# 48 modulation units: weighted sums of weight chunks on VectorE and a sum over partitions on TensorE, in place of matrix products

## The chip, the cores and the metric

One core (a NeuronCore) of one Trainium2 chip runs the whole kernel. The metric is the device time of one execution in microseconds; the median of three executions of the kernel before is 2996.09 us (2994.24 to 2999.81). The profile is of one further execution.

## The reference, cut to what matters

The program is a two-layer block with modulated norms, followed by a second two-layer block that the change does not touch. In each layer of the first block, two condition vectors (`c` and `c_ctx`, 1024 values each) give nine modulation vectors each:

```
def _modulation(cond, w, b):
    m = jax.nn.silu(cond) @ w + b        # w is 1024 x 9216
...
sh1, sc1, g1, shm, scm, gm, sh2, sc2, g2 = _modulation(c, ada_w[layer], ada_b[layer])
csh1, csc1, cg1, cshm, cscm, cgm, csh2, csc2, cg2 = _modulation(c_ctx, ada_w[layer], ada_b[layer])
h = h + 0.5 * g1 * _swiglu(_prenorm(h, norm_ffn1[layer], sh1, sc1), ffn1_w_in[layer], ffn1_w_out[layer])
...
h = h + gm * (mix_l @ mix_w_out[layer])
h = h + 0.5 * g2 * _swiglu(_prenorm(h, norm_ffn2[layer], sh2, sc2), ffn2_w_in[layer], ffn2_w_out[layer])
```

`_swiglu` is a feed-forward stage: first products (`h @ w_in`, the gate and the other half), silu of the gate times the other half, second products (`@ w_out`).

## The kernel before, in words

**Products.** Activations lie with features on partitions, 256 latent and 256 context tokens beside each other (512 columns). Every float32 product is done as three matmuls of the type fp32r: high part times high part, low times high, high times low (`three`, L470 to L472). Weights come through the double-buffered tile `raw` in *units*: a unit is one slot `s` (0 or 1) with two halves. SP loads each half (L379), ScalarE copies it to the high part `whi` (L412), VectorE subtracts to get the low part `wlo` (L419), TensorE multiplies. The semaphores `lo_ready`, `mm_done` and `evac_done` link them, so that loads run about two units ahead and splits one unit ahead. `pairs_of` (L422) writes the loop over pairs of units for each compute engine: in each unit first `before`, then `ahead` (the split of the next unit), then the body.

**A feed-forward stage** (`ffn`, one function for each engine) goes over the 22 blocks of 128 hidden features in two parts of 12 and 10 (`HALVES`). A part has first products (`up`, one unit for each hidden block: 8 chunks x 2 x 3 = 48 matmuls of 512 columns) and second products (`down`, 8 units, that is four pairs). In an `up` unit ScalarE takes the silu of the gate (L2065), VectorE multiplies (L2749), ScalarE copies the high part of the hidden block (L2068), VectorE subtracts for the low part (L2753). In `down` VectorE adds the product, scaled by the modulation, to `hT` (L2800).

**Modulation units.** A layer's 9216 modulation columns are 36 units of 256 columns, 72 in all. Eight are computed in the opening, 16 in three stretches about the norms (`MOD_AT_NORM`), and 48 beside the products of the feed-forward stages (`MOD_BESIDE`): in feed-forward 1 and feed-forward 2 of layer 0, in six groups of 5, 4, 1, 5, 4 and 5 pairs of units, beside `up` and `down` pairs. These 48 are the subject. For each, SP loads 1 MB of `ada_w` into a slot of `mod_w` (L723) as soon as TensorE is through with that slot. At the start of a pair of product units, TensorE waits for both loads and runs `mod_rows_of` (L558) for both slots: for each of eight chunks of 128 input features one float32 matmul, with 32 columns of `cond` (the two conditions, placed so that they meet the rows of this unit) as the loaded operand and 256 weight columns streaming. The eight go by turns to the four groups of 32 rows of the PSUM bank 6. At a group's end VectorE copies the bank to `mod_row` (L2623), TensorE turns rows to columns (`mod_turned`, L565), which also adds the four row groups, and VectorE adds the bias (L2546).

**Order on SP's queue.** `sp_units` (L369) issues, for each unit, the two halves of `raw`, each behind its wait, and then the modulation load of this slot with its own wait (`mod_unit`, L718). In the last `down` of a stage `mods_at_norm` puts one load for the next norm behind each pair.

Of the kernel before, what the change touches and what calls it, by code (L numbers as in the profile page):

```python
# [26 lines left out]
P = 128  # L27
D = 1024
DC = D // P
T = 256  # L30
# [93 lines left out]
def build(nc, io, const_at):  # L124

    ctx = ExitStack()
    with ctx:
# [56 lines left out]
        out_at = first.at  # L184
        mod_w = first("mod_w", [P, 2, DC, 2 * P])
        mod_row = first("mod_row", [P, 2 * P])
        mod_w2 = first("mod_w2", [P, DC, 2 * P])
        mod_w3 = Region(out_at - 4 * 4 * 2 * T)("mod_w3", [P, DC, 2 * P])
        normed = Region(overlay)("normed", [P, DC, 2 * T])
# [359 lines left out]
        def mod_landings(layer, m0):  # L549

            before = [part[2] for stage in ("ffn1", "ffn2") for part in beside_parts[stage] if part[:2] < (layer, m0)]
            return 16 * (sum(before) + 1)
# [9 lines left out]
        def mod_turned(row, bank):  # L562
# [5 lines left out]

        beside_parts = {stage: [part for part in MOD_BESIDE[stage] if part] for stage in ("ffn1", "ffn2")}
        mod_groups = [2] * (MOD_FIRST // 2) + [2 * part[2] for part in beside_parts["ffn1"]] + \  # L570
            [MOD_AT_NORM[name][2] for name in ("mix", "ffn2")] + [2 * part[2] for part in beside_parts["ffn2"]] + \
            [MOD_AT_NORM["ffn1"][2]]
# [60 lines left out]
        none = (None,) * 4  # L633
        beside = {(stage, 0): mods for stage, mods in MOD_BESIDE.items()}
        for layer, mixer, w_in in ((0, "even", io["even_w_in"][0]), (1, "odd", io["odd_w_in"][0])):
# [10 lines left out]
                 beside.get(("ffn1", layer), none), False, PAIR if layer else OPENING,  # L646
# [8 lines left out]
                 beside.get(("ffn2", layer), none), False, 0 if layer else PAIR, None if layer else "ffn1"),  # L655
# [30 lines left out]
        def _(sp):  # L686
# [50 lines left out]
            def ffn(w_in, w_out, mods, opened, at_norm):  # L737
                v = w_in.rearrange("(c p) (g f) -> p c g f", p=P, g=2)
                j0 = 0
                for n, half in enumerate(HALVES):  # L740
# [4 lines left out]
                    for p0, pairs, mod_part in parts(half // 2, mods[2 * n], p_first):  # L745
                        sp_units(sp, c, pairs, up(p0), UNIT, mod_part and mod_unit(*mod_part))
                    if n == 1 and at_norm:
# [7 lines left out]
                    for p0, pairs, mod_part in parts(4, mods[2 * n + 1]):  # L755
                        sp_units(sp, c, pairs, columns(w_out, j0, half, 2 * p0 * P, P, P), half * P,
                                 mod_part and mod_unit(*mod_part))
# [114 lines left out]
        def _(pe):  # L872
# [41 lines left out]
            def opening():  # L914
# [51 lines left out]
                for t in range(1, (n_rows + P - 1) // P):  # L966
# [6 lines left out]
                    .then_inc(S("bcast_mm"), 1)  # L973

            def mod_unit(layer, m0, pairs):
                group = mod_group(layer, m0)
                def rows_first(i, s):
                    if s:
                        return
                    if i == 0:  # L980
                        pe.wait_ge(S("mod_copied"), group)
                    for slot in range(2):
                        pe.wait_ge(S(f"mod_landed{slot}"), 16 * i + mod_landings(layer, m0))
                        mod_rows_of(mod_w[:, slot, :, :], 6, 2 * i + slot, 2 * pairs).then_inc(S("mod_rows_mm"), 1)
# [1518 lines left out]
        def _(dve):  # L2503
# [227 lines left out]
            def ffn(n_tok, final, mods, gate, scaled=False, opened=0, at_norm=None, turned=None):  # L2731
                for n, half in enumerate(HALVES):
# [34 lines left out]
                    for p0, pairs, mod_part in parts(half // 2, mods[2 * n], p_first):  # L2767
# [5 lines left out]
                        if mod_part:  # L2773
                            mod_read(*mod_part, pairs)
# [847 lines left out]
```

## Time and profile before

| | |
|---|---|
| median of three runs | 2996.09 us |
| the profiled execution's own time | 2992.23 us |
| its span, first to last instruction | 2990.5 us |
| TensorE matmul, busy | 2932.5 us, 98% |
| VectorE, busy | 1690.7 us, 57% |
| ScalarE, busy | 1314.1 us, 44% |
| moved by DMA | 439.36 MB, mean 147 GB/s |

The profiled execution took 1.7 us more than its span. Matmuls are pipelined, so a matmul's listed duration is longer than the distance from one start to the next; costs on TensorE are best read from distances of starts.

### The profile page before, as it was taken

Reading aid. Unit: us, or ns where it says so; the run is one execution under the profiler, and the core shown is the slowest. Engines: PE = TensorE matmul, PEld = TensorE weight load, DVE = VectorE, ACT = ScalarE, POOL = GpSimd, SP = SyncE. Lnnn points to the kernel's source line nnn. Section 1 sums busy time; section 2 is a strip of 40 time slices with the busy share of each in tenths; the row PEclk is TensorE's granted clock in tenths of the full one; section 3 lists DMA queues with packets and bytes.
Section 4 is the critical chain, followed back from the end, with each engine's and each line's share of the span. In section 5 each row is a group of like instructions: output and inputs, shape, how many; then the busy total and the mean of one; then the engine's idle time right before and its main releaser. Section 6 shows DMA issues by size and latency. Waiting matters only on the chain.

```text
span 2990.5 us, 52037 instructions
## 1 busy us (share of the span) xinstructions
PE 2932.5 (98%) x20172; PEld 2580.5 (86%) x20172; DVE 1690.7 (57%) x2664; ACT 1314.1 (44%) x1952; POOL 0.2 (0%) x4
## 2 busy tenths in 40 slices
PE   9999999999999999999998999999999999999999
PEld 6778878787777878888888999999899999988998
DVE  4333363545332453334666667677776776777766
ACT  4322343423222342223335656555555555556555
POOL 0000000000000000000000000000000000000000
PEclk9999999999999999999999999999999999999999
DMA  9555343146566433332322666455446654554564
GB/s 275 181 176 148 89 154 93 43 149 176 166 202 181 141 113 95 95 105 76 121 85 79 190 184 186 132 156 170 141 141 196 175 156 146 166 164 139 163 191 137
DMA packets 639011, 439.36 MB, mean 147 GB/s; under 512 B 22172, under 2 KB 627192, under 8 KB 638712
## 3 DMA queue, kind: packets, MB, share of 16 engines
q1 hardware_dynamic: 637844, 436.70, 49.1%
q8 instruction: 125, 2.05, 0.3%
q14 instruction: 46, 0.38, 0.0%
q10 hardware_dynamic: 996, 0.23, 0.0%
HBM read 430.84 MB, written 1.05 MB: 144 GB/s over the span
## 4 chain that ended last, share of the span: by engine, by line
PE 87%; DVE 8%; ACT 1%; issue 1%; SPq 1%; DMA 1%; DVEq 0%; ACTq 0%
PE ps L470 26%; PE ps L472 25%; PE ps L471 25%; DVE wlo L419 2%; PE ps L558 2%; ACT whi L412 1%; DMA raw<-ffn_w_in 1%; PE ps L1809 1%; DVE normed L2684 1%; PE ps L1789 1%; SPq L734 1%; PE ps L1821 1%; DVE xl L2676 1%; PE ps L1270 0%; PE ps L1279 0%
## 5 line engine op out<-in xcount | busy, mean ns | idle before, releaser
L470 PE MATMUL ps<-xh,whi 128*128 128x256 f32 (+1 forms) x3744 | 1204.8, 322 | 24.4 <-DVE wlo L419 5.6
L471 PE MATMUL ps<-xl,whi 128*128 128x256 f32 (+1 forms) x3744 | 1183.7, 316 | 0.0
L472 PE MATMUL ps<-xh,wlo 128*128 128x256 f32 (+1 forms) x3744 | 1183.6, 316 | 0.0
L419 DVE TENSOR_TENSOR wlo<-raw,whi 128x1024 fp32r<-128x1024 f32 x732 | 869.1, 1220 | 182.7 <-ACT whi L412 174.5
L412 ACT ACTIVATE whi<-raw 128x1024 fp32r<-128x1024 f32 x731 | 747.4, 1053 | 462.1 <-PE ps L472 398.9
L470 PEld LDWEIGHTS ps<-xh,whi 128*128 128x128 f32 x3744 | 705.4, 188 | 106.5 <-issue 45.0
L472 PEld LDWEIGHTS ps<-xh,wlo 128*128 128x128 f32 x3744 | 705.6, 188 | 50.6
L471 PEld LDWEIGHTS ps<-xl,whi 128*128 128x128 f32 x3744 | 706.3, 189 | 48.6
L470 PE MATMUL ps<-hid_h,whi 128*128 128x512 f32 (+1 forms) x1056 | 353.4, 335 | 0.0
L471 PE MATMUL ps<-hid_l,whi 128*128 128x512 f32 (+1 forms) x1056 | 352.3, 334 | 0.0
L472 PE MATMUL ps<-hid_h,wlo 128*128 128x512 f32 (+1 forms) x1056 | 352.2, 334 | 0.0
L2749 DVE TENSOR_TENSOR hid<-act,ps 128x512 f32<-128x512 f32 (+1 forms) x132 | 73.2, 554 | 440.0 <-PE ps L472 429.0
L2068 ACT ACTIVATE hid_h<-hid 128x256 f32 (+3 forms) x132 | 69.3, 525 | 426.2 <-DVE hid L2749 426.2
L470 PEld LDWEIGHTS ps<-hid_h,whi 128*128 128x128 f32 x1056 | 198.8, 188 | 23.9 <-issue 3.3
L472 PEld LDWEIGHTS ps<-hid_h,wlo 128*128 128x128 f32 x1056 | 198.5, 188 | 20.7
L471 PEld LDWEIGHTS ps<-hid_l,whi 128*128 128x128 f32 x1056 | 198.2, 188 | 20.4
L2800 DVE SCALAR_TENSOR_TENSOR hT<-ps,mod,hT 128x256 f32 (+1 forms) x112 | 49.8, 480 | 212.8 <-PE ps L472 212.4
L2753 DVE TENSOR_TENSOR hid_l<-hid,hid_h 128x256 f32 (+3 forms) x132 | 73.8, 559 | 105.6 <-ACT hid_h L2068 105.6
L2065 ACT ACTIVATE act<-ps 128x512 f32<-128x512 f32 (+1 forms) x88 | 47.5, 540 | 148.7 <-PE ps L472 148.6
L470 PE MATMUL ps<-whi,xh 128*128 128x256 f32 x384 | 110.7, 288 | 0.1
L472 PE MATMUL ps<-whi,xl 128*128 128x256 f32 x384 | 107.5, 280 | 0.0
L471 PE MATMUL ps<-wlo,xh 128*128 128x256 f32 x384 | 107.5, 280 | 0.0
(380 smaller groups left out, 2593.9 us busy)
## 6 DMA issues: line engine op xcount, KB each, us to landing
raw<-ffn_w_in SPq DMA_DIRECT2D x176, 512.0 KB, 4.7
mod_w<-ada_w SPq DMA_DIRECT2D x72, 1024.0 KB, 7.7
raw<-w_in SPq DMA_DIRECT2D x96, 512.0 KB, 4.6
raw<-w_ffn_in SPq DMA_DIRECT2D x88, 512.0 KB, 4.7
raw<-w_gate SPq DMA_DIRECT2D x64, 512.0 KB, 4.1
raw<-ffn_w_out SPq DMA_DIRECT2D x64, 384.0 KB, 3.9
raw<-ffn_w_out SPq DMA_DIRECT2D x64, 320.0 KB, 3.6
raw<-w_branch SPq DMA_DIRECT2D x32, 512.0 KB, 3.4
```

The source lines that it names most:

```text
L412: nc.scalar.activation(split_at(unit_of(u, i), whi, s, h), raw[:, s, h, :], ACT.Copy).then_inc(S("hi_ready"), 1)
L419: nc.vector.tensor_tensor(split_at(unit, wlo, s, h), raw[:, s, h, :], split_at(unit, whi, s, h).bitcast(F32), ALU.subtract).then_inc(S("lo ...
L470: nc.tensor.matmul(dst, w_h, x_h, start=start, stop=False)
L471: nc.tensor.matmul(dst, w_h, x_l, start=False, stop=False)
L472: return nc.tensor.matmul(dst, w_l, x_h, start=False, stop=stop)
L558: m = nc.tensor.matmul(ps[g, bank, 0:2 * P], cond[:, k, 30 - 2 * j:62 - 2 * j], w[:, k, :], start=j == 0 and k < 4, stop=j == n - 1 and k ...
L734: sp.dma_start(norm_tiles[name][j], mod_columns((MOD_UNITS * layer + m0 + j) // MOD_UNITS, (m0 + j) % MOD_UNITS))\
L2065: nc.scalar.activation(act32[:, s, 0:n_tok], gate_in, ACT.Silu).then_inc(S("act_ready"), 1)
L2068: nc.scalar.activation(hid_h[:, bass.ds(i * 2 + (hid0 + s), 1), 0:n_tok], hid32[:, s:s + 1, 0:n_tok], ACT.Copy).then_inc(S("hid_h_ready"), 1)
L2749: nc.vector.tensor_tensor(hid32[:, s, 0:n_tok], act32[:, s, 0:n_tok], ps[:, 2 * s + 1, 0:n_tok], ALU.mult).then_inc(S("evac_done"), 1)
L2753: nc.vector.tensor_tensor(hid_l[:, to, 0:n_tok], hid32[:, s:s + 1, 0:n_tok], hid_h[:, to, 0:n_tok].bitcast(F32), ALU.subtract)\
L2800: ins = nc.vector.scalar_tensor_tensor(out=hT[:, to, sl], in0=ps[:, 2 * s:2 * s + 1, sl], scalar=mod[:, bass.ds(i * 2 + (gate0 + n0 + s), ...
```

## The change

The 48 units are computed by another route, and all of them beside *first* products: five pairs in each part of feed-forward 1 and of feed-forward 2 of layer 0, and four pairs in the first part of feed-forward 1 of layer 1. Which units are computed about the third norm is changed to suit (24 to 27 of layer 1 in place of 32 to 35).

For a pair of units (512 weight columns), SP loads half of the input features of both units at a time (`mod_pair`, again 1 MB for each DMA, 48 in all, now with runs of 512 columns). VectorE multiplies each of the eight chunks by the condition's value of that partition and adds, once for each condition: 16 instructions of 128x512 for a pair, eight in each unit of the product pair, four before the split of the next unit and four after it. TensorE then multiplies the accumulated tiles by a column of ones: four matmuls for a pair. Their place is one pair later, ahead of its second unit; the last pair's are ahead of the first `down` unit, and the rows are turned ahead of the second.

```
-MOD_BESIDE = {"ffn1": ((0, 8, 5), (0, 18, 4), (0, 26, 1), None),
-              "ffn2": ((1, 4, 5), (1, 14, 4), (1, 22, 5), None)}
-MOD_AT_NORM = {"mix": (0, 28, 4, 3, 4), "ffn2": (0, 32, 8, 5, 6), "ffn1": (1, 32, 4, 3, 4)}
+MOD_BESIDE = {("ffn1", 0): ((0, 8, 5), (0, 18, 5)), ("ffn2", 0): ((1, 4, 5), (1, 14, 5)), ("ffn1", 1): ((1, 28, 4), None)}
+MOD_AT_NORM = {"mix": (0, 28, 4, 3, 4), "ffn2": (0, 32, 8, 5, 6), "ffn1": (1, 24, 4, 3, 4)}
+MOD_STEPS = 2 * DC
...
+        mod_sel = first("mod_sel", [P, 2 * 32])
+        mod_pair = Region(mod_w_at)("mod_pair", [P, DC, 4 * P])
+        mod_acc = Region(mod_acc_at)("mod_acc", [P, 2, 2, 4 * P])
```

In the stream of SP:

```
             def mod_unit(layer, m0):
...
+                sp.wait_ge(S("mod_rows_mm"), MOD_UNITS * layer + m0)
+                before = c.of["mod_pairs"]
                 def load(i, s):
-                    sp.wait_ge(S("mod_rows_mm"), 2 * i + (MOD_UNITS * layer + m0 + s - 1))
-                    sp.dma_start(mod_w[:, s, :, :], mod_columns(layer, i * 2 + (m0 + s))).then_inc(S(f"mod_landed{s}"), 16)
+                    sp.wait_ge(S("mod_step"), i * MOD_STEPS + mod_summed(before - 1, DC * (s + 1)))
+                    sp.dma_start(mod_pair[:, s * DC // 2:(s + 1) * DC // 2, :], mod_pair_columns(layer, i * 2 + m0, s))\
+                        .then_inc(S(f"mod_landed{s}"), 16)
```

In the stream of TensorE (the former `rows_first` and `turned` go):

```
             def mod_unit(layer, m0, pairs):
...
+                def rows(pair):
+                    if pair == 0:
+                        pe.wait_ge(S("mod_copied"), group)
+                    pe.wait_ge(S("mod_step"), mod_summed(before + pair, MOD_STEPS))
+                    for u in range(2):
+                        for j in range(2):
+                            to, g = 2 * (2 * pair + u) + j, 32 * (2 * u + j)
+                            m = nc.tensor.matmul(ps[g:g + 32, 6, 0:2 * P], mod_sel[:, 31 - to:63 - to],
+                                                 mod_acc[:, pair % 2, j, u * 2 * P:(u + 1) * 2 * P],
+                                                 start=pair == 0, stop=pair == pairs - 1)
+                    m.then_inc(S("mod_rows_mm"), 2)
+                def rows_before(i, s):
+                    if s == 1 and i:
+                        rows(i - 1)
```

In the stream of VectorE:

```
+            def mod_sums(layer, m0):
...
+                def sums(i, s, part):
+                    pair = before + i
+                    if part == 0:
+                        dve.wait_ge(S(f"mod_landed{s}"), 16 * (pair + 1))
+                    if s == 0 and part == 0:
+                        dve.wait_ge(S("mod_rows_mm"), MOD_UNITS * layer + m0 + max(0, 2 * (i - 1)))
+                    for k in range(4 * s + 2 * part, 4 * s + 2 * part + 2):
+                        for j in range(2):
+                            acc, weight = mod_acc[:, i % 2, j, :], cond[:, k, 30 + j:31 + j]
+                            if k == 0:
+                                ins = nc.vector.tensor_scalar(acc, mod_pair[:, k, :], weight, None, ALU.mult)
+                            else:
+                                dve.wait_ge(S("mod_step"), mod_summed(pair, 2 * k + j - 1))
+                                ins = nc.vector.scalar_tensor_tensor(out=acc, in0=mod_pair[:, k, :], scalar=weight,
+                                                                     in1=acc, op0=ALU.mult, op1=ALU.add)
+                            ins.then_inc(S("mod_step"), 1)
```

VectorE runs `sums(i, s, 0)` as `before` of each `up` unit and `sums(i, s, 1)` at the start of its body, ahead of the multiplication L2749. At the first `down` unit it copies the rows, waits for the turned ones, adds the bias, and halves the gate. Two memsets prepare `mod_sel` in each stage. The waits of SP for `mod_rows_mm` now stand at the entry of a group, ahead of the raw loads of its first pair.

## Rows read from the trace of the kernel before

**Rows 1.** The page: busy us (share) xinstructions, and the granted clock.
```profile
PE 2932.5 (98%) x20172; PEld 2580.5 (86%) x20172; DVE 1690.7 (57%) x2664; ACT 1314.1 (44%) x1952; POOL 0.2 (0%) x4
...
PEclk9999999999999999999999999999999999999999
```
**Rows 2.** The page: the chain of work that ended last, by engine.
```profile
PE 87%; DVE 8%; ACT 1%; issue 1%; SPq 1%; DMA 1%; DVEq 0%; ACTq 0%
```
**Rows 3.** Groups by shape, TensorE: busy us, mean ns | idle before.
```profile
L558 PE MATMUL ps<-mod_w,cond 128*32 128x256 f32 x1152 | 70.0, 383 | 1.4 <-DMA mod_w<-ada_w 1.4
```
**Rows 4.** Timeline of VectorE, feed-forward 1: start us, us, instruction [idle before].
```profile
109.23 0.69 DVE L2749 TENSOR_TENSOR hid<-act,ps 128x512 f32<-128x512 f32 x1 [6.07 <-PE ps L472]
110.84 0.69 DVE L2753 TENSOR_TENSOR hid_l<-hid,hid_h 128x512 f32 x1 [0.92 <-ACT hid_h L2068]
...
133.08 0.69 DVE L2749 TENSOR_TENSOR hid<-act,ps 128x512 f32<-128x512 f32 x1 [6.08 <-PE ps L472]
...
171.49 0.69 DVE L2753 TENSOR_TENSOR hid_l<-hid,hid_h 128x512 fp32r<-128x512 f32 x1 [0.80 <-ACT hid_h L2068]
172.09 0.42 DVE L2623 COPY mod_row<-ps 128x256 f32<-128x256 f32 x1
```
**Rows 5.** The same view in layer 1, no modulation beside.
```profile
1129.32 0.69 DVE L2749 TENSOR_TENSOR hid<-act,ps 128x512 f32<-128x512 f32 x1 [6.07 <-PE ps L472]
...
1131.77 2.36 DVE L419 TENSOR_TENSOR wlo<-raw,whi 128x1024 fp32r<-128x1024 f32 x2
...
1151.08 0.69 DVE L2749 TENSOR_TENSOR hid<-act,ps 128x512 f32<-128x512 f32 x1 [6.07 <-PE ps L472]
```
**Rows 6.** Timeline of TensorE: groups of 4, 16 and 32 small matmul records.
```profile
49.59 0.39 PE L472 MATMUL ps<-xh,wlo 128*128 128x512 f32 x1
49.82 0.53 PE L565 MATMUL ps<-consts,mod_row 128*128 128x32 f32 x4
50.18 0.48 PE L470 MATMUL ps<-xh,whi 128*128 128x512 f32 x1
...
62.29 1.07 PE L558 MATMUL ps<-mod_w,cond 128*32 128x256 f32 x16 [0.76 <-DMA mod_w<-ada_w]
63.29 0.50 PE L470 MATMUL ps<-xh,whi 128*128 128x512 f32 x1
...
85.28 1.93 PE L558 MATMUL ps<-mod_w,cond 128*32 128x256 f32 x32
87.14 0.50 PE L470 MATMUL ps<-xh,whi 128*128 128x512 f32 x1
```
**Rows 7.** Groups by shape, VectorE: nearest forms to the new instructions.
```profile
L3055 DVE SCALAR_TENSOR_TENSOR o_p<-o_p,o_st 128x512 f32<-128x512 f32 x12 | 9.0, 752 | 0.4
...
L3053 DVE TENSOR_SCALAR o_p<-o_p,o_st 128x512 f32<-128x512 f32 x12 | 5.8, 487 | 0.4
```
**Rows 8.** Timeline of VectorE: spacing of unchained instructions, and (last) of chained ones.
```profile
34.71 1.26 DVE L2572 SCALAR_TENSOR_TENSOR normed<-hT,gains,ps 128x256 f32<-128x256 f32 x3
...
1522.60 0.75 DVE L3055 SCALAR_TENSOR_TENSOR o_p<-o_p,o_st 128x512 f32<-128x512 f32 x1
1523.27 1.22 DVE L3062 TENSOR_REDUCE o_st<-ps 128x2 f32<-128x1024 f32 x1
...
1863.63 1.51 DVE L3199 SCALAR_TENSOR_TENSOR m_cv<-m_in,vec,m_cv 128x255 f32<-128x255 f32 x3
```
**Rows 9.** All instructions of `mod_w`: landing of its loads.
```profile
DMA to landing us min/median/max: 5.0/7.7/12.3
```
**Rows 10.** Timeline of SP's queue in the opening: start, time over the group.
```profile
33.69 6.02 SPq L379 DMA_DIRECT2D raw<-ffn_w_in  x2
48.61 0.37 SPq L723 DMA_DIRECT2D mod_w<-ada_w  x1
```
**Rows 11.** Timeline of ScalarE, first split of the first unit after the opening.
```profile
55.57 1.06 ACT L412 ACTIVATE whi<-raw 128x1024 fp32r<-128x1024 f32 x1
```
**Rows 12.** The page: DMA issues of `raw`, KB each, us to landing.
```profile
raw<-ffn_w_in SPq DMA_DIRECT2D x176, 512.0 KB, 4.7
```

More of the change, by code:

```diff
@@ L631, in build @@
         schedule = []
-        none = (None,) * 4
-        beside = {(stage, 0): mods for stage, mods in MOD_BESIDE.items()}
+        none = (None,) * 2
         for layer, mixer, w_in in ((0, "even", io["even_w_in"][0]), (1, "odd", io["odd_w_in"][0])):
@@ L754, in ffn @@
                         continue
-                    for p0, pairs, mod_part in parts(4, mods[2 * n + 1]):
-                        sp_units(sp, c, pairs, columns(w_out, j0, half, 2 * p0 * P, P, P), half * P,
-                                 mod_part and mod_unit(*mod_part))
+                    sp_units(sp, c, 4, columns(w_out, j0, half, 0, P, P), half * P)
                     j0 += half
@@ L972, in opening, with rest @@
                 nc.tensor.matmul(ps[:, 5, 64:128], K("ones")[0:1, :], small_rows[0:1, :], start=True, stop=True)\
-                    .then_inc(S("bcast_mm"), 1)
+                    .then_inc(S("vec_t"), 1)
             def mod_unit(layer, m0, pairs):
-                group = mod_group(layer, m0)
-                def rows_first(i, s):
-                    if s:
-                        return
[L980 to L984, printed above, removed]
-                def turned(i, s):
-                    if i == pairs - 1 and s == 1:
+                group, before = mod_group(layer, m0), c.of["mod_pairs"]
+                c.add(mod_pairs=pairs)
+                def rows(pair):
[12 more added lines that the diff above has]
+                        rows(i - 1)
+                def rest(i, s):
+                    if not isinstance(i, int) or i:
+                        return
+                    if s == 0:
+                        rows(pairs - 1)
+                    else:
                         pe.wait_ge(S("mod_copied"), group + 1)
@@ L2766, in ffn @@
                         late_vectors()
-                    for p0, pairs, mod_part in parts(half // 2, mods[2 * n], p_first):
+                        dve.wait_ge(S("cond"), 1)
+                    if mods[n] and n == 0:
+                        link(nc.vector.memset(mod_sel[:, :], 0.0))
+                        link(nc.vector.memset(mod_sel[:, 31:32], 1.0))
+                    for p0, pairs, mod_part in parts(half // 2, mods[n], p_first):
                         hid0 = 2 * p0
                         split_done = n == 0 and not gate
+                        sums = mod_sums(*mod_part) if mod_part else None
@@ new lines, in ffn, with down @@
+                    add = add_gated(gate, n_tok // T, 0) if gate else add_plain(n, 0)
+                    def down(i, s):
+                        if mods[n] and is_first(i, s):
+                            mod_copy_and_read(mods[n][0], mods[n][1], mods[n][2])
+                            if n == 0:
+                                gate_halved()
+                        unit_done(dve, c, i, s)
+                        add(i, s)
+                        if n == 1:
+                            sq_lag(i, s, 1, n_tok)
@@ L2791, in ffn @@
+                    pairs_of(dve, c, 4, down, ahead=dve_split, final=final and n == 1, first=n == 1 or bool(mods[n]))
                 sq_close(1, n_tok)
```

107 lines of the change are left out of this document (52 added, 55 removed).

## The prediction

> **What bounds the kernel now.** I read the busy shares first: TensorE is busy 98% of the span, at a granted clock in the top tenth in every slice (the 2.4 GHz level), while VectorE has 43% free [rows 1]. The chain of waits says the same: 87% of it lies on TensorE [rows 2]. So whatever leaves TensorE's stream comes off the time, unless another engine then makes it wait. The groups by shape show what the change takes hold of: 1152 records of L558, 70 us busy, only 1.4 us of waiting for their loads [rows 3]. They are 72 units of 8 matmuls with 2 records each; the 48 units in question are 768 of them.
>
> **What a pair of units costs TensorE now.** The timeline of VectorE is a clean ruler, since L2749 starts when a unit of products ends. Over one pair with modulation it goes from 109.23 to 133.08, 23.85 us [rows 4]; over one without, from 1129.32 to 1151.08, 21.76 us [rows 5]. A pair of units costs 2.09 us, of which 1.86 is seen directly (85.28 to 87.14, 32 records [rows 6]) and 0.23 is the change-over to and from the fp32r products. 24 pairs: 50.2 us, all on the path. The pair after the opening also waits 0.76 us for its load [rows 6].
>
> **What a pair costs TensorE after.** 4 matmuls of the same shape, 8 records, one in each of the same four row groups. The trace has no group of 8. Sixteen records take 1.00 us to the next product (62.29 to 63.29), thirty-two 1.86 [rows 6], so one more record is 0.054 us and eight would be 1.86 - 24 x 0.054 = 0.57; with the change-over of 0.23, 0.80. From below the bound is a quarter of 2.09, 0.52; from above the 16-record group with change-over, 1.23. I take 0.80, between rows of the same shape: 19.2 us for 24 pairs (12.5 to 29.5). Groups beside products fall from six to five, so one turning of 4 records goes: 49.82 to 50.18, 0.4 us [rows 6]. Sum on TensorE: -50.2 - 0.8 + 19.2 - 0.4 = **-32.2 us** (-22 to -39).
>
> **What VectorE gets.** For each pair 2 multiplications by a scalar and 14 multiply-and-add of 128x512. Nearest rows: 752 ns for the same operation and width, 487 ns for the multiplication [rows 7]. They overlap by some 0.08 us: the 752 ns instruction is followed 0.67 us later, and three unchained ones of 256 columns take 1.26 us where the three chained in m_cv take 1.51, 0.12 us more for each link [rows 8]. The new sums alternate between two accumulators and wait only for the last but one, which is done by then; I take 0.67 and 0.40: 14 x 0.67 + 2 x 0.40 = 10.2 us a pair, 5.1 a unit, 5.4 where all eight are sums. Fully chained it would be 0.79 each, 6.3 a unit. From below, 0.67 is already the spacing of an unhindered one.
>
> The Trainium skill has a rule that speaks against counting on the overlap: "VectorE: DVE Perf Modes", section "The DRAIN you can't avoid", says that the next operation does not start until the pipe is empty, and that semaphores cost nothing extra. By that rule a sum would take its full 0.75 us, some 6.0 us for eight. The trace disagrees in both halves (0.67 apart, and 0.12 for a link [rows 8]); the verdict below holds at either price.
>
> A unit's round on VectorE: L2749 to L2753 1.61 us (109.23 to 110.84), L2753 to the next 0.60 [rows 4], the two splits 2.36 [rows 5], together 4.6; with 5.4 of sums 10.0 us. TensorE's round is 10.88 us (half of 21.76), 11.28 with half of the 0.80. VectorE would be near 90% busy in these stretches, but still the faster one. Order matters as well as sum. With t=0 where TensorE ends the last unit: L2749 and L2753 until 2.2, four sums until 4.9, the splits until 7.3, four sums until 10.0, then the wait for the unit's end at 10.9 or 11.7. The next unit's split is due at 10.9, so 3.6 us of slack; fully chained sums leave 3.1. The first two chunks of a row group are needed a unit later. Only a group's last pair is short: TensorE wants it right at the end of the last `up` unit (11.7), VectorE is done at 10.0; chained, 10.9. Cost nil in both.
>
> **Loads and SP's queue.** Still 48 DMAs of 1 MB, in place of L723's. Each half of `mod_pair` is a single buffer: it is reloaded when its eight sums are done (t=10.0 of one unit) and wanted two units on, at 2.2: 22.6 + 2.2 - 10.0 = 14.8 us, against a landing of 7.7 us in the median and 12.3 at most [rows 9]. On SP the raw loads of a slot stand behind the modulation load before them, hence are issued near t=10 instead of t=7.3; ScalarE wants them a unit later, landing takes 4.7 us [rows 12]. Nil. The new wait at a group's entry holds raw loads back: those of the first unit after the opening were issued at 33.69 and now follow at about 48.6, where the wait for the rows is released [rows 10]. Landed by 48.6 + 0.5 + 4.7 = 53.8, they precede ScalarE's split at 55.57 [rows 11]; if that cover of 1.8 us is gone, each further us is a us once. At the last `down` of two stages the modulation loads now wait for rows made at the first `down` unit, and the raw load behind them too; the unit they serve is two `down` units away, 13.6 us (30 matmuls each at 10.88/48). Later groups' waits are long fulfilled. After the opening VectorE comes late to the second unit's split, behind two memsets and the first four sums (2 x 0.40 + 2 x 0.67 = 2.1 us): between nothing and 2.1 us once, and I count 0.5, since TensorE has a whole unit of 10.9 us to run first. At the first `down` unit VectorE waits for the turned rows, until just after that unit's end; its split is done before, and the bank is wanted only a unit (8.2 us, 36 matmuls) later. Nil. TensorE's first `down` row groups are in the 24. What is late next, after the removed wait for a load, is the split.
>
> **Sum.** -32.2 + 0.5 = -31.7 us on the execution profiled: 2992.2 to 2960.5. The median of the runs shown stands 3.9 us higher, so by it 2964.4; I say **2964**. A measurement of this kernel can tell about 0.2%, 6 us, from no change.
>
> **The rivals.**
>
> *Small row groups cost more than their records* (chance 0.08). If 8 records cost like 16, the pair costs 1.23 and the sum is -21.5: 2974. For it: entering from fp32r costs something regardless of size. Against: the 4-record group took only 0.36 us [rows 6].
>
> *VectorE falls a little behind* (0.14). The sums stand ahead of split and L2749. It decides where a sum takes more than (11.28 - 4.6) / 8 = 0.84 us. At 0.90 a round is 11.8 and each of some 46 units loses 0.5: 23 us of the gain, 2987 (2970 to 2994). For it: such a density of dependent 512-column work is nowhere in the trace. Against: 0.79 even when chained.
>
> *The loads become the bound, and it is slower* (0.09). The head of VectorE's queue now waits for the modulation load, and behind that wait stand the split and L2749, hence ScalarE and TensorE; before, TensorE alone waited. The loop is: load, sums over two sections with the split between (7.8 us), load again. The pair takes 22.6 us while the load lands within 14.8; each us beyond costs one for each of the 19 pairs that follow another in their group. It eats the whole gain at 16.5 us; at 18 us it is 3.2 x 19 - 32 = +29: **3025**. For it: the opening shows loads of up to 12.3 us. Against: the median of 7.7, and the same bytes in almost the same time.
>
> *As forecast* 0.69 (2957 to 2970).
>
> The change that doesn't do what it says (sums stay on TensorE) isn't possible by the diff; the nearest case is the first rival.
>
> **How the numbers follow.** The first two cases lie at 2957 to 2975 with 0.77; a mild lag of VectorE reaches to 2984, with some 0.07 of its 0.14. Below, the quarter bound gives -39, 2957. So 2956 to 2984 holds a bit over 8 in 10. Faster by over 0.2%: 0.69 + 0.08 + 0.10 of the lag = 0.87; within 0.2%: 0.04, the heavy end of the lag; slower: 0.09.
>
> **What would show it.** TensorE's small matmuls drop from 1152 records to 384 of the old form and 192 of the new; their new groups take about 0.57 us to the next product. L2749 starts 22.6 us apart over two units. The new sums are 750 ns long and 0.67 apart; VectorE's busy time rises by some 24 x 11.5 = 276 us (durations, less the overlap). Idle of L470 on `wlo` L419 stays where it was: if it grows by more than 5 us, the lag is real. If VectorE's first sum of a section waits for the `mod_pair` load, the third rival is at work. A time above 2984 would say that I misjudged a wait on VectorE.

## The result, and the profile after

| | before | changed |
|---|---|---|
| median, runs on the same chip | 2997.79 us (2994.24 to 2999.81) | 2969.7 us (2962.13 to 2971.68, four runs) |
| the profiled execution | 2992.23 us, span 2990.5 | 2962.13 us, span 2960.3 |

The ratio of the times is 0.9908, with a 95% interval of 0.9895 to 0.9922: by it 27.6 us less (23.4 to 31.5). The two profiled executions are 30.1 us apart; both are fast ones, that of before faster than the four runs of the table, that of the changed kernel the fastest of its four. The forecast was 31.7 us less for the profiled execution and 2964 for the median; the measured median is 5.7 us above that and inside the range.

The page of the changed kernel: the span, busy us and counts as in [rows 1], the chain by engine as in [rows 2], and the new issue of loads (KB each, us to landing).

```profile
span 2960.3 us, 51063 instructions
...
PE 2901.3 (98%) x19592; PEld 2559.7 (86%) x19592; DVE 1928.7 (65%) x3052; ACT 1314.6 (44%) x1952; POOL 0.2 (0%) x4
...
PE 86%; DVE 8%; ACT 2%; issue 1%; SPq 1%; DMA 1%; DVEq 0%; ACTq 0%
...
mod_pair<-ada_w SPq DMA_DIRECT2D x48, 1024.0 KB, 5.3
```

TensorE is busy 31.2 us less and still 98% of the span: what it lost came off the end. VectorE gained 238 us of work and the chain's share on it stayed at 8%. The groups by shape (busy us, mean ns | idle before) show where both sit; the first line answers to [rows 3].

```profile
L566 PE MATMUL ps<-mod_w,cond 128*32 128x256 f32 x384 | 23.7, 390 | 0.3 <-DMA mod_w<-ada_w 0.3
...
L995 PE MATMUL ps<-mod_acc,mod_sel 128*32 128x256 f32 x192 | 15.3, 391 | 0.0
...
L2656 DVE SCALAR_TENSOR_TENSOR mod_acc<-mod_pair,cond,mod_acc 128x512 f32<-128x512 f32 x336 | 230.7, 746 | 0.0
...
L2653 DVE TENSOR_SCALAR mod_acc<-mod_pair,cond 128x512 f32<-128x512 f32 x48 | 21.0, 481 | 0.1
```

Old records: 384 instead of 1152. New ones: 192, and the engine never stood idle for them (0.0). The sums took 746 ns and never waited for a load either; the multiplications ahead of them waited 0.1 us in all. One new group in TensorE's timeline, answering to [rows 6]:

```profile
91.40 0.39 PE L477 MATMUL ps<-xh,wlo 128*128 128x512 f32 x1
91.72 0.64 PE L995 MATMUL ps<-mod_acc,mod_sel 128*32 128x256 f32 x8
92.29 0.50 PE L475 MATMUL ps<-xh,whi 128*128 128x512 f32 x1
```

From the group's start to the next product it is 92.29 - 91.72 = 0.57 us, the interpolated value. VectorE's timeline over a pair (L2788 is the former L2749, L2792 the former L2753, L424 the split), as in [rows 4]:

```profile
91.93 0.69 DVE L2788 TENSOR_TENSOR hid<-act,ps 128x512 f32<-128x512 f32 x1 [1.53 <-PE ps L477]
...
94.03 2.74 DVE L2656 SCALAR_TENSOR_TENSOR mod_acc<-mod_pair,cond,mod_acc 128x512 f32<-128x512 f32 x4
96.68 2.35 DVE L424 TENSOR_TENSOR wlo<-raw,whi 128x1024 fp32r<-128x1024 f32 x2
98.95 2.73 DVE L2656 SCALAR_TENSOR_TENSOR mod_acc<-mod_pair,cond,mod_acc 128x512 f32<-128x512 f32 x4
103.61 0.69 DVE L2788 TENSOR_TENSOR hid<-act,ps 128x512 f32<-128x512 f32 x1 [1.93 <-PE ps L477]
...
114.49 0.69 DVE L2788 TENSOR_TENSOR hid<-act,ps 128x512 f32<-128x512 f32 x1 [1.66 <-PE ps L477]
```

From 91.93 to 114.49 is 22.56 us: 21.76 of products [rows 5] and 0.80 for the new group with its change-over. VectorE's own work in a round is 103.61 - 1.93 - 91.93 = 9.75 us, after which it waits for TensorE. The forecast had 10.0.

**Where the time went, by stage.** The view of windows, us of the stretch first; then busy us of TensorE matmul, its loads, VectorE, ScalarE and GpSimd, granted clock, DMA share and GB/s. The stretches are: opening and feed-forward 1 of layer 0; the mixer; its output product with the norm sum; feed-forward 2 of layer 0; feed-forward 1 of layer 1. Before:

```profile
0.00:425.00 425.00, 417.52 (x2223) 331.46 (x2227) 164.88 (x233) 142.94 (x176) 0.20 (x4) 1.00 0.58 176
425.00:635.10 210.10, 202.71 (x1513) 172.23 (x1506) 108.32 (x215) 80.12 (x116) 0.00 (x0) 1.00 0.19 57
635.10:680.70 45.60, 45.22 (x270) 36.02 (x272) 20.81 (x34) 11.74 (x17) 0.00 (x0) 1.00 0.93 277
680.70:1079.40 398.70, 397.93 (x2168) 316.13 (x2160) 153.05 (x207) 118.61 (x149) 0.00 (x0) 1.00 0.57 172
1079.40:1448.90 369.50, 366.46 (x1637) 302.72 (x1627) 150.64 (x200) 117.72 (x148) 0.00 (x0) 1.00 0.32 94
```

Changed:

```profile
0.00:409.80 409.80, 403.20 (x1977) 322.55 (x1980) 263.83 (x393) 142.90 (x176) 0.20 (x4) 1.00 0.62 182
409.80:621.50 211.70, 204.34 (x1513) 173.34 (x1506) 108.31 (x215) 80.12 (x116) 0.00 (x0) 0.99 0.19 56
621.50:668.60 47.10, 45.29 (x271) 36.07 (x273) 20.83 (x34) 11.76 (x17) 0.00 (x0) 1.00 0.81 246
668.60:1047.90 379.30, 378.46 (x1796) 305.13 (x1788) 252.15 (x368) 119.16 (x149) 0.00 (x0) 1.00 0.54 158
1047.90:1420.90 373.00, 370.04 (x1669) 303.42 (x1662) 190.83 (x267) 117.63 (x147) 0.00 (x0) 1.00 0.41 119
```

Differences: -15.2, +1.6, +1.5, -19.4, +3.5, and -2.2 over the rest of the kernel, which the change does not touch; together -30.2. That rest took 1541.8 us before and between 1539.5 and 1548.6 us in the profiled executions of the changed kernel and its variants, so -2.2 is scatter, and some 9 us of scatter lie there. By the forecast's own prices the three feed-forward stages should give:

- first (10 pairs by the new route where 10 were by the old, one turning less, the load wait of 0.76 gone, +0.5 in the opening): -10 x 1.29 - 0.4 - 0.76 + 0.5 = -13.6;
- second (10 by the new where 14 were by the old): 10 x 0.80 - 14 x 2.09 - 0.4 = -21.7;
- third (4 new, one turning more): 4 x 0.80 + 0.4 = +3.6.

The third fits to 0.1 us. What the other stretches differ by has three causes, which the traces show.

*Short drops of the granted clock.* The mean clock of such long stretches is too coarse for them. In slices of 5 us both traces have some. One slice of before (25 to 30 us) and two stretches of the changed kernel:

```profile
25.00:30.00 5.00, 4.57 (x19) 2.73 (x22) 0.64 (x2) 1.36 (x2) 0.00 (x0) 0.67 1.10 303
```

```profile
520.00:530.00 10.00, 10.00 (x35) 7.29 (x35) 5.53 (x8) 7.08 (x9) 0.00 (x0) 0.83 0.35 107
665.00:675.00 10.00, 8.11 (x77) 5.25 (x70) 6.63 (x16) 5.66 (x11) 0.00 (x0) 0.83 0.01 2
```

The 0.67 and 0.83 are the granted clock: part of the slice at the 1.2 GHz level. As an estimate from them, each costs up to (1 - 0.67) x 5 or (1 - 0.83) x 10 = 1.7 us. The other profiles bear the first two out. The mixer took 211.7 or 211.8 us in the five profiles that had one such drop in it, 213.3 in the one with two, and 210.1 or 210.2 us in the others: this is the mixer's +1.6. The first stage took 409.2 to 410.1 us in the changed kernel and in every variant whose work there is the same and that had no drop at 25 us; the one of experiment 2 with ten sums had it (0.68) and took 411.6 us. Before had it, and so lost the 1.6 us by which the changed kernel did better than the forecast. The third drop lies at the start of the second feed-forward stage; the kernel of experiment 5, without a drop there, took 378.3 us for that stage, 1.0 less.

*The first pair of a stage was cheaper than 2.09 us.* Also without the drop, the second stage is some 1.3 us short of the forecast (378.3 - 398.7 = -20.4 instead of -21.7). TensorE's timeline at the start of the feed-forward stage, in the kernel before with modulation beside, before in layer 1 with none, and in the changed kernel:

```profile
707.58 1.93 PE L558 MATMUL ps<-mod_w,cond 128*32 128x256 f32 x32
709.45 0.50 PE L470 MATMUL ps<-xh,whi 128*128 128x512 f32 x1
```

```profile
1107.21 0.49 PE L470 MATMUL ps<-xh,whi 128*128 128x512 f32 x1 [0.84 <-DVE hid L2749]
```

```profile
697.22 0.50 PE L475 MATMUL ps<-xh,whi 128*128 128x512 f32 x1 [0.76 <-DVE hid L2788]
```

Where nothing else is to be done there, TensorE waits about 0.8 us for `hid`. The old matmuls of the group's first pair stood in that wait: they took 1.86 us and spared 0.84, so they cost 1.0 us and taking them away gave back 1.0, not 2.09. That explains 1.1 of the 1.3 us.

*The norm's sums come later.* In the stretch of the output product TensorE waits for them (waits: total us, times, longest), in the changed kernel

```profile
PE ps L1044 <- DVE ss L2546: 1.8, 1, 1.8
```

where the kernel before has

```profile
PE ps L1023 <- DVE ss L2524: 0.4, 1, 0.4
```

These 1.4 us are the stretch's +1.5. On VectorE's queue the split of the next stage's weights stands ahead of the norm's last sums. It waits for ScalarE's copy, and that for the load of `raw`. ScalarE's waits in that stretch, before and changed:

```profile
ACT whi L412 <- DMA raw<-ffn_w_in: 4.2, 2, 3.5
```

```profile
ACT whi L417 <- DMA raw<-ffn_w_in: 5.7, 2, 4.9
```

So the load reaches ScalarE 1.5 us later in relation to the products, and all behind it is late by as much. Counted from the end of the stretch's products, SP issued it 0.6 us later; why, and where the other 0.9 us come from, no run shows. The drop at 665 to 675 us follows TensorE's wait: of the twelve profiles with a wait of 1.6 to 2.0 us there, ten have a drop behind it, and the kernel before, with 0.4 us, has none.

### The profile page after: what moved, and what is told of

Same layout as the page of the kernel before. It is cut to its first block, busy times and chain, and to the rows that moved or that the text cites. A ratio compares the mean times of both kernels' runs of the same rounds, so it can differ in the third digit from the quotient of the medians.

```text
span 2960.3 us, 51063 instructions
## 1 busy us (share of the span) xinstructions
PE 2901.3 (98%) x19592; PEld 2559.7 (86%) x19592; DVE 1928.7 (65%) x3052; ACT 1314.6 (44%) x1952; POOL 0.2 (0%) x4
## 4 chain that ended last, share of the span: by engine, by line
PE 86%; DVE 8%; ACT 2%; issue 1%; SPq 1%; DMA 1%; DVEq 0%; ACTq 0%
PE ps L475 27%; PE ps L477 25%; PE ps L476 25%; DVE wlo L424 2%; ACT whi L417 1%; DMA raw<-ffn_w_in 1%; PE ps L1831 1%; PE ps L1811 1%; SPq L744 1%; DVE normed L2721 1%; PE ps L1843 1%; DVE xl L2713 0%; PE ps L566 0%; PE ps L995 0%; PE ps L1292 0%
## 5 line engine op out<-in xcount | busy, mean ns | idle before, releaser
L424 DVE TENSOR_TENSOR wlo<-raw,whi 128x1024 fp32r<-128x1024 f32 x732 | 868.4, 1220 | 169.7 <-ACT whi L417 167.1
L417 ACT ACTIVATE whi<-raw 128x1024 fp32r<-128x1024 f32 x731 | 747.6, 1054 | 448.5 <-PE ps L477 379.7
L2656 DVE SCALAR_TENSOR_TENSOR mod_acc<-mod_pair,cond,mod_acc 128x512 f32<-128x512 f32 x336 | 230.7, 746 | 0.0
L2788 DVE TENSOR_TENSOR hid<-act,ps 128x512 f32<-128x512 f32 (+1 forms) x132 | 73.2, 554 | 202.5 <-PE ps L477 191.5
L2792 DVE TENSOR_TENSOR hid_l<-hid,hid_h 128x256 f32 (+3 forms) x132 | 73.8, 559 | 99.5 <-ACT hid_h L2090 99.5
```

The source lines that it names most:

```text
L417: nc.scalar.activation(split_at(unit_of(u, i), whi, s, h), raw[:, s, h, :], ACT.Copy).then_inc(S("hi_ready"), 1)
L424: nc.vector.tensor_tensor(split_at(unit, wlo, s, h), raw[:, s, h, :], split_at(unit, whi, s, h).bitcast(F32), ALU.subtract).then_inc(S("lo ...
L2656: ins = nc.vector.scalar_tensor_tensor(out=acc, in0=mod_pair[:, k, :], scalar=weight, in1=acc, op0=ALU.mult, op1=ALU.add)
L2788: nc.vector.tensor_tensor(hid32[:, s, 0:n_tok], act32[:, s, 0:n_tok], ps[:, 2 * s + 1, 0:n_tok], ALU.mult).then_inc(S("evac_done"), 1)
L2792: nc.vector.tensor_tensor(hid_l[:, to, 0:n_tok], hid32[:, s:s + 1, 0:n_tok], hid_h[:, to, 0:n_tok].bitcast(F32), ALU.subtract)\
```

## The experiments

Ratios are to the kernel before, run beside each kernel on the same chip, with 95% intervals. The changed kernel was taken again as a control, as it is:

> The changed kernel once more, as the measure for the run of paired rows beside it: 0.991 of the kernel before, as when it was first measured (0.9908).

2967.64 us (2965.92 to 2970.38, five runs), 0.9913 [0.9899, 0.9926]. Its stretches were 410.1, 210.1, 46.9, 380.0 and 373.0 us, against the 409.8, 211.7, 47.1, 379.3 and 373.0 of the first profile.

**1. Are the sums hidden?** They keep number, order and waits and are cut to one column. This leaves out all but the first of their columns, for chunks 1 to 7.

```
-ins = nc.vector.scalar_tensor_tensor(out=acc, in0=mod_pair[:, k, :], scalar=weight,
-                                     in1=acc, op0=ALU.mult, op1=ALU.add)
+ins = nc.vector.scalar_tensor_tensor(out=acc[:, 0:1], in0=mod_pair[:, k, 0:1], scalar=weight,
+                                     in1=acc[:, 0:1], op0=ALU.mult, op1=ALU.add)
```

> The 14 multiply-and-add instructions of each pair work on one column in place of 512 (so 511 of 512 columns of the modulation sums hold only the first chunk's product); all semaphores, loads and TensorE's matmuls stay. Theory (VectorE's sums are wholly hidden behind TensorE's products): the same time as the changed kernel, span 2960 +-2, L2788 still starts 22.6 us apart over two units. Rival (VectorE lags a little and some of the 32 us expected on TensorE is lost to it): faster than the changed kernel by 2 to 10 us, and TensorE's idle before the first matmul of a unit, 9.7 us for the 128x512 form, falls.

2966.25 us, 0.9911 [0.9893, 0.9929]. The group, then two instructions of VectorE's timeline:

```profile
L2656 DVE SCALAR_TENSOR_TENSOR mod_acc<-mod_pair,cond,mod_acc 128x1 f32<-128x1 f32 x336 | 51.7, 213 | 0.0
```

```profile
91.48 0.69 DVE L2788 TENSOR_TENSOR hid<-act,ps 128x512 f32<-128x512 f32 x1 [4.13 <-PE ps L477]
...
103.16 0.69 DVE L2788 TENSOR_TENSOR hid<-act,ps 128x512 f32<-128x512 f32 x1 [6.19 <-PE ps L477]
```

179 us less of work on VectorE turned into waiting for TensorE (4.1 and 6.2 us instead of 1.5 and 1.9), with no time gained. The median is 1.4 us under the control's and 3.5 under the changed kernel's first one, which is scatter: the five stretches are 409.3, 211.7, 47.0, 379.7 and 373.0 us, none more than 0.5 us off the changed kernel's, and TensorE's idle time before the first matmul of a unit, which the rival had falling, went from 9.7 to 10.1 us. The sums cost nothing. The rival in which VectorE lags is out at eight sums.

**2. Where does it begin to cost?** Further sums of the same form into the same accumulators: two in each unit (ten in all), or four (twelve), half of them ahead of the split. Their weight is a column of zeros, so the accumulated values stay, and only VectorE's work grows.

```
+MOD_EXTRA = 2
-MOD_STEPS = 2 * DC
+MOD_STEPS = 2 * DC + 2 * MOD_EXTRA
...
+dve.wait_ge(S("mod_step"), mod_summed(pair, n - 1))
+nc.vector.scalar_tensor_tensor(out=acc, in0=mod_pair[:, ks[0], :], scalar=cond[:, ks[0], 0:1],
+                               in1=acc, op0=ALU.mult, op1=ALU.add).then_inc(S("mod_step"), 1)
```

> Two more multiply-and-add of 128x512 in each unit (weight zero, so nothing changes in the result), ten in place of eight. From the changed kernel's trace a unit on VectorE is 2.1 us of hid work, 2.3 of splits and 0.66 for each sum: 11.0 us with ten sums (10.7 on average, the two multiplications of a pair being shorter), against TensorE's 11.28. Theory: still hidden, +0 to +3 us on the changed kernel. Rival (what stands in front on VectorE's queue costs, sum by sum): +15 us or more (48 units x 2 x 0.66 = 63 at worst).

> Four more multiply-and-add of 128x512 in each unit (weight zero), twelve in place of eight. A unit on VectorE becomes 12.1 us on average against TensorE's 11.28. Theory: past the crossing, some 0.8 us for each of 48 units less the slack of each group's first units, +25 to +37 us on the changed kernel, so level with the kernel before or a little slower (span 2985 to 2997), with TensorE idle before L475 on wlo or hid. Rival (sums cost nothing whatever their number, or each costs its full length): +0, or +127 us.

Ten: 2967.86 us, 0.9907 [0.9889, 0.9926], still free. Twelve: 3017.54 us, 1.0075 [1.0053, 1.0096]: slower than the kernel before, 48 us above the changed one and 50 above the control; the expectation of +25 to +37 was too low. VectorE's timeline with ten (L2798 is L2788 moved down):

```profile
96.47 0.68 DVE L2798 TENSOR_TENSOR hid<-act,ps 128x512 f32<-128x512 f32 x1
...
107.45 0.68 DVE L2798 TENSOR_TENSOR hid<-act,ps 128x512 f32<-128x512 f32 x1
...
117.90 0.68 DVE L2798 TENSOR_TENSOR hid<-act,ps 128x512 f32<-128x512 f32 x1
...
150.93 0.69 DVE L2798 TENSOR_TENSOR hid<-act,ps 128x512 f32<-128x512 f32 x1 [0.51 <-PE ps L478]
```

No wait stands behind the first three lines: VectorE goes at its own pace, 10.98 and 10.45 us a round (the second has the two cheaper multiplications), mean 10.7. TensorE needs 11.28 on average, so VectorE, which starts the stage late behind its first sums, catches up by 1.1 us a pair, and from 150.93 on it waits for TensorE again. The lag cost nothing: less its drop of the clock, the stage took the control's 410 us. With twelve the rounds are 12.31 and 11.79, mean 12.05, 0.77 us too long, and nothing is caught up. Over some 46 units that would be 35 us. TensorE's waits with twelve:

```profile
PE ps L996 <- DVE mod_acc L2658: 24.7, 4, 6.2
PE ps L476 <- DVE wlo L425: 20.7, 29, 1.5
```

The first line did not exist in the changed kernel; the second stood there at 8.8 us, 11.9 less. Together 36.6 us, the lag as worked out. The two profiled spans are further apart, 3014.6 - 2960.3 = 54.3 us. TensorE stood idle for 41.3 us more (the 36.6 and some smaller waits), and the same 19592 matmul records kept it busy for 13.0 us more, 2914.3 instead of 2901.3. The second part goes with the clock. The end of one group and the stretch behind it:

```profile
183.55 1.08 PE L996 MATMUL ps<-mod_acc,mod_sel 128*32 128x256 f32 x8 [6.20 <-DVE mod_acc L2658]
```

```profile
180.00:190.00 10.00, 6.45 (x26) 4.60 (x27) 7.48 (x11) 2.52 (x3) 0.00 (x0) 0.66 0.39 112
```

TensorE stood idle for 6.20 us, and the 10 us around it show a clock of 0.66; a slice at a lower clock stands at each of the four such waits. (1 - clock) x 5 us, summed over all slices of 5 us, gives 22.1 us, where the changed kernel's profile has 10.5. The 11.6 more are an upper estimate, since part of such a slice was idle anyway; the busy time is the better measure. The lag of a group's units gathers unseen, since buffers and a split a unit ahead cover it, and two thirds of it is paid at one place, the group's last rows, which are wanted at once.

**3. What does a small row group cost?** The four matmuls once more, with a column of zeros as the second loaded operand.

```
+for u in range(2):
+    for j in range(2):
+        g = 32 * (2 * u + j)
+        m = nc.tensor.matmul(ps[g:g + 32, 6, 0:2 * P], mod_sel[:, 32:64],
+                             mod_acc[:, pair % 2, j, u * 2 * P:(u + 1) * 2 * P],
+                             start=False, stop=pair == pairs - 1)
```

> Each pair's four row matmuls are followed by four more with an all-zero weight, in the same four row groups: 16 records for a pair in place of 8. Theory (price by records, 0.054 us each, plus 0.23 change-over for a group): +0.43 us for each of 24 pairs, +10.4 us on the changed kernel, each group 1.00 us to the next product. Rival (a group's price is its start and end, records overlap in the four row groups): +0 to +3 us. Other rival (eight matmuls cost twice four): +0.8 x 24 = +19 us.

2979.43 us, 0.9944 [0.9926, 0.9962]: 9.7 us above the changed kernel's median and 11.8 above the control's, or 0.41 to 0.49 us for each of 24 pairs (the forecast's slope: 8 x 0.054 = 0.43). A pair takes 12.15 + 10.88 us between starts of the multiplication, 0.47 more than in the changed kernel (11.68 + 10.88). In the timeline:

```profile
92.29 0.64 PE L995 MATMUL ps<-mod_acc,mod_sel 128*32 128x256 f32 x8
92.75 0.61 PE L1001 MATMUL ps<-mod_acc,mod_sel 128*32 128x256 f32 x8
93.29 0.50 PE L475 MATMUL ps<-xh,whi 128*128 128x512 f32 x1
```

Sixteen records take 1.00 us to the next product, as in [rows 6]. The price of records is straight, and eight records do not cost like sixteen: the first rival is out.

**4. The change-over by itself.** Rows of two pairs made together, every second pair, with a third pair of accumulators in a tile that is free there. The work is the same, the visits to TensorE's stream fewer: three instead of five in a group of five pairs, two instead of four in a group of four, 10 fewer in all.

```
+def acc_of(pair, j):
+    return sq2[:, j, :] if pair % 3 == 2 else mod_acc[:, pair % 3, j, :]
...
-if s == 1 and i:
+if s == 1 and i and i % 2 == 0:
+    rows(i - 2)
     rows(i - 1)
```

> The changed kernel with the row matmuls of two pairs run together: a third pair of accumulators lies in the tile of the squares, and TensorE runs rows of pairs 0 and 1 ahead of the second unit of the third pair, and so on; two groups of 8 records become one of 16. Theory (0.23 change-over and a tail for each group, 0.054 us for each record): 1.23 us in place of 2 x 0.80, 0.37 saved ten times, -3.7 us on the changed kernel; span 2956. Rival: nothing, if the price goes by records alone; slower, if two pairs' rows at once make the copy or the loads late.

2962.5 us (2960.94 to 2964.38), 0.9888 [0.9867, 0.9908]. The gain is of the size of the scatter between sets of runs, so it was measured again beside the control:

> The kernel with the row matmuls of two pairs run together, again, on the same chip as the changed kernel. By the price found in the traces (8 records 0.80 us, 16 records 1.23) ten merged groups save 3.7 us: 0.12% under the changed kernel, ratio 0.9895 to 0.990 if that one is at 0.991. Rival: the first look's 0.9888 against 0.9908 was scatter, and both come out the same.

2962.25 us (2961.29 to 2964.01, four runs), 0.9890 [0.9875, 0.9905], against the control's 2967.64, and the two sets of runs do not overlap. VectorE's timeline (L2794 is L2788 moved down), without rows and with those of two pairs:

```profile
102.61 0.69 DVE L2794 TENSOR_TENSOR hid<-act,ps 128x512 f32<-128x512 f32 x1 [1.12 <-PE ps L477]
113.49 0.69 DVE L2794 TENSOR_TENSOR hid<-act,ps 128x512 f32<-128x512 f32 x1 [1.66 <-PE ps L477]
125.64 0.69 DVE L2794 TENSOR_TENSOR hid<-act,ps 128x512 f32<-128x512 f32 x1 [2.39 <-PE ps L477]
```

A visit of sixteen records costs 12.15 - 10.88 = 1.27 us (the forecast's prices give 1.23), against 2 x 0.80 = 1.60 for two of eight: 10 x 0.33 = 3.3 us. The three feed-forward stretches are 1.8, 3.0 and 0.6 us shorter than the control's, 5.4 in all. Of the 3.0, some 1.7 are a clock drop at 665 us, which the control's profile has and this one has not: against the 378.3 us of experiment 5, also without a drop, this stage (377.0) is 1.3 us shorter. That leaves 1.8 + 1.3 + 0.6 = 3.7 us for the merging. This version beats both kernels.

**5. The spacing of the sums.** Each sum waits for the one just before instead of the last but one.

```
-dve.wait_ge(S("mod_step"), mod_summed(pair, 2 * k + j - 1))
+dve.wait_ge(S("mod_step"), mod_summed(pair, 2 * k + j))
```

> The changed kernel, but each sum waits for the one directly before it, in place of the last but one. Theory: each start is 0.12 us later, 0.78 apart in place of 0.66, a unit on VectorE 10.6 us against 11.28, still hidden: +0 to +2 us on the changed kernel. If the pipe is emptied between instructions anyway, the distance of starts does not change at all.

2967.14 us, 0.9908 [0.9887, 0.9929]. VectorE's timeline:

```profile
94.19 3.11 DVE L2656 SCALAR_TENSOR_TENSOR mod_acc<-mod_pair,cond,mod_acc 128x512 f32<-128x512 f32 x4
```

Four sums last 3.11 us, so with 0.75 for the last they start (3.11 - 0.75) / 3 = 0.787 apart; unchained, (2.74 - 0.75) / 3 = 0.663. A link costs 0.12 us, and here it is hidden. The Trainium skill, "VectorE: DVE Perf Modes", section "The DRAIN you can't avoid", has the next operation start only when the pipe is empty, and finds that a semaphore costs nothing extra. The same section adds an exception that the prediction left out: a next operation that is not held starts earlier. The 0.663 us, less than the 0.75 of one sum, goes with the exception; the 0.12 us of a link goes against the sentence on semaphores.

**6. The places alone.** The old matmuls at the new places, beside first products only.

```
-MOD_BESIDE = {"ffn1": ((0, 8, 5), (0, 18, 4), (0, 26, 1), None),
-              "ffn2": ((1, 4, 5), (1, 14, 4), (1, 22, 5), None)}
+MOD_BESIDE = {"ffn1": ((0, 8, 5), None, (0, 18, 5), None),
+              "ffn2": ((1, 4, 5), None, (1, 14, 5), None)}
+MOD_LATE = ((1, 28, 4), None, None, None)
```

> The kernel before with only the places changed: the 48 units are still computed by eight matmuls each on TensorE, but all beside first products, in the changed kernel's groups (5, 5, 5, 5 and 4 pairs) and with its assignment about the third norm. Theory (the gain is the price of the matmuls taken from TensorE, not the place): within 3 us of the kernel before (-0.4 for one turning less), span 2987 to 2993. Rival (part of the gain comes from taking modulation out of the second products and the loads with them): faster than before by 5 us or more.

2997.95 us, 1.0011 [0.9999, 1.0023]. The move itself brings nothing, perhaps costs 3 us. The gain is that of the new route. Its output product takes 47.1 us, and TensorE waits 1.9 us there for the norm's sums (ScalarE 5.8 us for the `raw` loads). So the +1.5 us there comes with the places, not with the sums. Every kernel with the new places shows it (46.8 to 47.8 us, against 45.6). The third feed-forward stage took 377.1 us, only 7.8 more than before for four old pairs and a turning: 3 x 2.09 + 0.4 and the first pair at 1.0, which is 7.7. TensorE's wait of 0.8 us for `hid` at that stage's start is gone in this kernel, which bears out the reading above.

**7. The wait at a group's entry on SP.** The wait for the rows is put where it was, ahead of the group's first modulation load and behind the raw loads.

```
-sp.wait_ge(S("mod_rows_mm"), MOD_UNITS * layer + m0)
 def load(i, s):
+    if not first_load:
+        first_load.append(1)
+        sp.wait_ge(S("mod_rows_mm"), MOD_UNITS * layer + m0)
```

> The changed kernel with SP's wait for the former rows moved from the entry of a group to its first modulation load, so that the raw loads of the group's first unit (and, at the last second products of a stage, nothing else) go out as early as before: in the opening near 34 us in place of 47. Theory: no effect, +-1 us, since these loads were covered. Rival (holding them back gave the loads of the opening more of the DMA, which would be the 1.7 us by which the opening was shorter in the changed kernel's trace): the opening is 1.7 us longer again.

2968.43 us, 0.9908 [0.9884, 0.9932]. SP's queue in the opening, in the changed kernel and in this one:

```profile
46.96 1.04 SPq L384 DMA_DIRECT2D raw<-ffn_w_in  x2
```

```profile
32.88 6.02 SPq L384 DMA_DIRECT2D raw<-ffn_w_in  x2
```

The loads go out 14 us earlier and the first stretch stays at 409.3 us (409.8). The delay is covered, and holding these loads back is not what shortened the stage.

**8. The loads.** The 1 MB load in two of 0.5 MB, with runs of 256 columns instead of 512.

```
-sp.dma_start(mod_pair[:, s * DC // 2:(s + 1) * DC // 2, :], mod_pair_columns(layer, i * 2 + m0, s))\
-    .then_inc(S(f"mod_landed{s}"), 16)
+for u in range(2):
+    sp.dma_start(mod_pair[:, s * DC // 2:(s + 1) * DC // 2, 256 * u:256 * u + 256],
+                 v[:, s * DC // 2:(s + 1) * DC // 2, bass.ds((i * 2 + m0 + u) * 256, 256)])\
+        .then_inc(S(f"mod_landed{s}"), 16)
```

> The changed kernel, but each load of 1 MB is issued as two of 0.5 MB with runs of 256 columns (1 KB) in place of 512 (2 KB). Theory (a load has 14.8 us to land and its length is hidden): the same time, +-1 us, while landing goes up from 5.3 us. Rival (the longer runs are part of the gain, by easing the raw loads' way): slower by 2 us or more, TensorE or VectorE waiting for mod_pair or raw.

2965.26 us, 0.9902 [0.9887, 0.9918]. Landing of the loads of `mod_pair`, in the changed kernel and in this one (minimum, median, maximum):

```profile
DMA to landing us min/median/max: 5.1/5.3/10.1
```

```profile
DMA to landing us min/median/max: 3.6/4.7/8.4
```

No effect on the time, and the landing of one DMA did not rise, as I had expected of shorter runs, but fell, each now moving half as much. The longest landing of the changed kernel, 10.1 us, is below the 14.8 us that a load has by the prediction. No run made it longer than that, so the third rival is out for this kernel, and the price that it put on later loads is not tested.

## Why the prediction was right, point by point

- **TensorE bounds the kernel; what leaves it comes off.** Right: 31.2 us less busy, 30.2 us less span, 98% busy in both. The exception is the first pair of the second feed-forward stage: its matmuls stood in a wait, and 1.1 us of their 2.09 did not come off.
- **A pair costs 0.80 us instead of 2.09.** Right to the digits that the ruler gives (0.57 in the timeline, 22.56 for a pair), and the slope by experiment 3. The stage without any old pair fits to 0.1 us. What was too high is "all on the path" for each of the 24 old pairs.
- **VectorE's round of 10.0 us under TensorE's 11.28.** Right: 9.75. Its busy time rose by 238 us, not by 276. The new instructions' own group times sum to 230.7 + 21.0 = 252 us, since busy time in a group counts overlapping stretches once, while I had multiplied 11.5 us of listed durations by 24; the other 14 us are not explained. The point from which it decides was put at 0.84 us a sum, 6.7 us of sums in a unit. Ten sums (6.7 us) are free and twelve (8.0) are not, as that says. But the price beyond the point was too low: one us for one us, twelve would cost 35, and they cost 48 to 50. What the clock takes behind the long waits was missing.
- **A group's last pair is the short one.** Right in place: with twelve sums all four waits of 6 us stand there, and with eight there is none.
- **Loads.** Right: no wait for them. They land in 5.3 us in the median. The 7.7 of the forecast was that of all 72 loads; the 48 of L723 alone had 7.0. The `raw` loads of `ffn_w_in` land later than before, 5.2 instead of 4.7 us.
- **SP's entry wait, nil.** Right by experiment 7; the raw loads went out at 46.96 (forecast: 48.6). My +0.5 us for the opening is too small to be told from nothing beside clock drops of 1.7 us.
- **The L424 wait stays.** Right: 8.8 us in 17 waits, against 8.6 in 17.
- **The Trainium skill's rule on VectorE's pipe.** The prediction gave it without the exception named in experiment 5, so the 0.67 us of the rows disagrees with less of it than the prediction says. The sum did not use the rule.
- **The sum of -31.7 us** was mis-sized by some 4 us against the medians (-27.6; the other runs with hidden sums gave ratios of 0.9902 to 0.9911, the control 0.9913). One term was missing and one was too high, 2.6 us together. The output product behind the mixer is some 1.5 us longer in every kernel with the new places: I listed the stages that hold the modulation, and not this one. And the first old pair of the second stage was worth 1.0 us, not 2.09. The clock drop behind the output product's wait adds about 1 us where it occurs. The rest is less than the runs of one kernel differ by, and no run settles it. That the two profiled executions come within 1.5 us of the forecast is in part luck: the kernel before had a drop in its first stage (1.6 us) and the rest of the kernel happened to be 2.2 us shorter. Against such scatter a sum of small terms can't be held to better than some 4 us.

## What to carry to other kernels

When one engine is busy 98% of the time, price the work taken off it by the distance of starts on an engine that follows it, and then ask for one number of the engine that takes the work: its round against the bound engine's round, which here was 9.75 against 11.28 us and left room for two more sums of 0.66. Test that margin by adding work, not only by removing it: eight, ten and twelve sums gave 0.9908, 0.9907 and 1.0075. Up to the margin a sum is free, beyond it every unit pays. Ask also where the removed work stood: in a wait it is worth only what it took beyond the wait. Once the work is small, how often it interrupts the stream of another type counts as well as its size: taking 10 of 24 visits away brought a further 3.3 us by the trace (5.4 between the medians).

## What had not been expected of the hardware

- Short drops of TensorE's granted clock to the 1.2 GHz level, in a kernel whose clock reads 0.99 to 1.00 in every long stretch. They recur at the same few places, in the changed kernel's time near 25, 520, 665, 1565, 1835 and 2415 us and at the end, but which of these have one differs from execution to execution. Where a stage could be compared with and without, a drop cost 1.0 to 1.7 us. Some follow an idle of 1.8 us (665), some follow nothing visible (520 to 530 us, 10.00 of 10.00 busy). With four idles of 6 us the matmuls took 13.0 us longer.
- Two orders of the same 512-column sums, 0.663 and 0.787 us apart, differ by the semaphore link alone.
- A small group of matmuls amid products of another type costs 0.80 us for eight records of 0.054 each, so 0.37 us for the visit itself (0.14 seen up to the next product's start, 0.23 only in the distance of L2788). A second group right behind the first costs 0.43 to 0.47, its records alone (0.57 to 1.00 us, and 11.68 to 12.15, in experiment 3).
